# Routed experts in a fused two-block kernel: turns of 128 and of 64 slots alternate in one loop body, and two weight tiles of each 64-slot turn are multiplied as plain fp32

## Reference

```
logits = (xt @ w_router).astype(jnp.float32)
top_vals, top_idx = lax.top_k(logits, TOP_K)                      # TOP_K = 2
top_w = jax.nn.softmax(top_vals, axis=-1)
combine = jnp.sum(jax.nn.one_hot(top_idx, N_EXPERTS) * top_w[..., None], axis=1)
y = jnp.zeros_like(xt)
for e in range(N_EXPERTS):                                        # 8 experts
    y = y + combine[:, e:e + 1] * swiglu(xt, w_gate[e], w_up[e], w_down[e])   # width 3584
```

## Time and profile before

| | us |
|---|---|
| three runs | 2570.8, 2575.92, 2578.6 (median 2575.92) |
| span of the profiled execution | 2569.7 |
| its expert turns (655.03 to 1564.75) | 909.72 |
| a large turn (turns 1, 2, 3) | 119.41 |
| turn 4, small, behind a large one | 105.65 |
| turns 5, 6, 7, small, behind a small one | 108.26, 108.33, 108.84 |

### The profile page before, as it was taken

The page is one execution under the profiler, slowest core; times in us unless marked ns, Lnnn a source line. Parts: engine busy times, 40 slices in busy tenths (PEclk is TensorE's granted clock), DMA queues, the critical chain, the costliest instruction groups (busy, mean ns, idle before and its releaser), DMA issues.

```text
span 2569.7 us, 32436 instructions
## 1 busy us (share of the span) xinstructions
PE 2384.0 (93%) x12064; PEld 1861.5 (72%) x12064; DVE 2009.7 (78%) x3035; ACT 1256.6 (49%) x1302; POOL 285.7 (11%) x305
## 2 busy tenths in 40 slices
PE   9999999999999999999899899999999987878786
PEld 8899999899788888877677678888985443323332
DVE  5766754865898888989999999666668887887875
ACT  2554332363777777878888886216421111111111
POOL 0000000000000000000000000000013433333341
PEclk9999999999999999999999999999999998899999
DMA  8454654541899999999999997531769999999997
GB/s 246 155 189 133 196 193 140 164 159 67 334 375 380 377 375 370 390 374 415 414 415 408 414 416 265 153 92 47 244 248 421 421 421 421 421 422 421 422 421 294
DMA packets 238447, 786.10 MB, mean 306 GB/s; under 512 B 24369, under 2 KB 154545, under 8 KB 162289
## 3 DMA queue, kind: packets, MB, share of 16 engines
q1 hardware_dynamic: 198000, 504.46, 53.1%
q0 software_dynamic: 39184, 276.58, 26.3%
q10 hardware_dynamic: 1136, 3.43, 0.3%
HBM read 777.08 MB, written 7.34 MB: 305 GB/s over the span
## 4 chain that ended last, share of the span: by engine, by line
PE 58%; DMA 22%; DVE 10%; issue 5%; ACT 4%; POOL 0%; DVEq 0%; ACTq 0%; SPq 0%
DMA dense_weights<-in_peer_rows,work 14%; DMA weight_tiles<-in_moe_tiles 7%; PE banks L862 7%; PE banks L864 7%; PE banks L863 7%; PE banks L728 5%; PE banks L1327 5%; PE banks L682 5%; PE banks L683 4%; PE banks L686 4%; PE banks L660 4%; DVE weight_tiles_low L2573 3%; ACT weight_tiles_high L1857 2%; PE banks L592 1%; PE banks L968 1%
## 5 line engine op out<-in xcount | busy, mean ns | idle before, releaser
L2573 DVE TENSOR_TENSOR weight_tiles_low<-weight_tiles,weight_tiles_high 128x2048 fp32r<-128x2048 f32 x335 | 761.5, 2288 | 72.7 <-ACT weight_tiles_high L1857 67.1
L1857 ACT ACTIVATE weight_tiles_high<-weight_tiles 128x2048 fp32r<-128x2048 f32 x332 | 635.5, 1918 | 149.4 <-DMA weight_tiles<-in_moe_tiles 144.7
L1327 PE MATMUL banks<-dense_weights,work 128*128 128x512 f32 x888 | 415.4, 618 | 57.9 <-DVE work L3104 57.5
L1327 PEld LDWEIGHTS banks<-dense_weights,work 128*128 128x128 f32 x888 | 173.0, 199 | 289.9 <-issue 201.1
L3094 DVE CUSTOM_DVE_ANT_0 dense_weights<-dense_weights,banks 128x1024 f32<-128x1024 f32 x222 | 266.5, 1217 | 68.2 <-DMA dense_weights<-in_peer_rows,work 67.3
L2205 DVE TENSOR_TENSOR weight_tiles_low<-weight_tiles,weight_tiles_high 128x2048 fp32r<-128x2048 f32 x93 | 212.2, 2289 | 129.2 <-ACT weight_tiles_high L1623 129.0
L2119 ACT ACTIVATE work<-work,small 128x2 f32<-128x2 f32 x129 | 38.1, 295 | 540.4 <-DVE work L3094 540.2
L1599 POOL DMA_INDIRECT dense_weights<-in_peer_rows,work x222 | 208.6, 940 | 588.0 <-DVE work L3050 315.0
L968 PE MATMUL banks<-weight_tiles_high,gathered_parts 128*128 128x512 f32 x448 | 183.8, 410 | 27.3 <-DVE weight_tiles_low L2573 26.8
L1623 ACT ACTIVATE weight_tiles_high<-weight_tiles 128x2048 fp32r<-128x2048 f32 x93 | 177.4, 1910 | 56.2 <-PE banks L864 29.5
L682 PE MATMUL banks<-weight_tiles_high 128*128 128x256 f32 x800 | 189.4, 281 | 5.1 <-issue 3.1
(11 more groups left out here) (508 smaller groups left out, 4467.9 us busy)
## 6 DMA issues: line engine op xcount, KB each, us to landing
weight_tiles<-in_moe_tiles SPq DMA_DIRECT2D x336, 1024.0 KB, 8.3
weight_tiles<-in_w_in SPq DMA_DIRECT2D x38, 1024.0 KB, 5.5
weight_tiles<-in_w_xkv SPq DMA_DIRECT2D x16, 1024.0 KB, 5.7
weight_tiles<-in_ffn_w_gate SPq DMA_DIRECT2D x11, 1024.0 KB, 5.3
weight_tiles<-in_ffn_w_up SPq DMA_DIRECT2D x11, 1024.0 KB, 5.3
weight_tiles<-in_ffn_w_down SPq DMA_DIRECT2D x11, 1024.0 KB, 5.0
weight_tiles<-in_w_xq SPq DMA_DIRECT2D x8, 1024.0 KB, 5.2
weight_tiles<-in_w_xo SPq DMA_DIRECT2D x8, 1024.0 KB, 5.2
```

The source lines that it names most:

```text
L1327: mm = pe.matmul(halves[half], diag[(first + j) % 8], pair_row(first + j)[:, 1, half * 512:(half + 1) * 512], start=False, stop=end and j ...
L1857: act.activation(high_tile(j), raw_tile(j), ACT.Copy).then_inc(g.high, 1)
L2573: dve.tensor_tensor(low_tile(j), raw_tile(j), high_tile(j).bitcast(F32), ALU.subtract).then_inc(g.split, 1)
```

## The change

1. The order of turns. Turns 0, 2, 4, 6 are large and 1, 3, 5, 7 small. The rank of an expert is turned into its turn: rank r < 4 goes to turn 2r, r > 3 to turn 2r - 7. That is two more small VectorE operations (128x8) ahead of `holds`.
2. The loops. One loop over three pairs, with a large and a small turn in its body, on TensorE, ScalarE and VectorE; the read of `extra_flag` behind it; and the fourth pair written out.
3. Two tiles of each small turn, number 11 (the last of the third gate-up chunk) and number 29 (the second of down), are *whole*: ScalarE and VectorE leave them out, TensorE waits for the raw tile itself and multiplies it as plain fp32, one `matmul` for each of the four pieces, in place of two fp32r ones. They add up in the same PSUM bank.
4. The gather of rows loads 128 rows in a small turn and 64 in a large one (the last turn's too, 128).
5. Counts of semaphores follow (`Turn.parts`, `rows_added`).

```diff
+NATIVE = (11, 29)
+PAIR_PARTS = 2 * EXP_TILES - len(NATIVE)
+class Turn:
+    def whole(self, j):
+        return self.small and j in NATIVE
+    def parts(self, j):
+        return self.parts_before + j + 1 - (sum(i <= j for i in NATIVE) if self.small else 0)
+    def following(self):
+        if self.pair is None:
+            return plain_turn(self.e + 1)
+        return large_turn(self.pair + 1) if self.small else small_turn(self.pair)
...
+                    def unsplit(j, rows_):
+                        pe.wait_ge(g.raw_loads[j % RING], g.loaded_before + 16 * (j // RING + 1) + e * (16 * EXP_TILES // RING))
+                        return raw_tile(j).rearrange("p (k n) -> p k n", k=rows_)
...
+                                    if t.whole(j):
+                                        mm = pe.matmul(bank, xe_high[:, k, :].bitcast(F32), whole[:, i, :], start=(k == 0), stop=(k == KT - 1))
+                                    elif small:
                                         mm = both(bank, xe_high[:, k, :], high[:, i, :], low[:, i, :], k == 0, k == KT - 1)
...
-                    with pe.Fori(0, LARGE) as e:
-                        turn(e, False)
+                    with pe.Fori(0, PAIRS - 1) as p:
+                        turn(large_turn(p))
+                        turn(small_turn(p))
                     pe.wait_ge(routing_ready, 1)
                     overflow = pe.value_load(extra_flag[0:1, 0:1], min_val=0, max_val=1)
-                    with pe.Fori(LARGE, N_EXP) as e:
-                        turn(e, True)
+                    turn(large_turn(PAIRS - 1))
+                    turn(small_turn(PAIRS - 1))
...
-                kind, m = "s_" if e >= LARGE else "", HALF if e + 1 >= LARGE else P
+                kind, m = ("s_", P) if e % 2 else ("", HALF)
...
-                def round_tile(e, j):
-                    wait_used(act, g, e, j)
+                def round_tile(t, j):
+                    if t.whole(j):
+                        return
+                    wait_used(act, g, t.e, j)
...
-                step.then(dve.tensor_tensor(holds, eight(rank, 1), eight(iota8, 2), ALU.is_equal))
+                step.then(dve.tensor_scalar(turn_back, rank, float(LARGE) - 0.5, -float(N_EXP - 1), ALU.is_gt, ALU.mult))
+                step.now(dve.scalar_tensor_tensor(turn_at, rank, 2.0, turn_back, ALU.mult, ALU.add))
+                step.then(dve.tensor_tensor(holds, eight(turn_at, 1), eight(iota8, 2), ALU.is_equal))
...
-                def low_part(e, j):
-                    dve.wait_ge(g.high, e * EXP_TILES + j + 1)
+                def low_part(t, j):
+                    if t.whole(j):
+                        return
+                    dve.wait_ge(g.high, t.parts(j))
                     dve.tensor_tensor(low_tile(j), raw_tile(j), high_tile(j).bitcast(F32), ALU.subtract).then_inc(g.split, 1)
...
-                with dve.Fori(0, LARGE - 1) as e:
-                    expert(e, True)
+                with dve.Fori(0, PAIRS - 1) as p:
+                    expert(large_turn(p), True)
+                    small_expert(small_turn(p), True)
```

More of the change, by code:

```diff
@@ L93, with __init__, large_turn, small_turn @@
 EXP_MARKS = 2 * CHUNKS + DOWN - 1
+PAIRS = N_EXP // 2
+NATIVE = (11, 29)
+PAIR_PARTS = 2 * EXP_TILES - len(NATIVE)
+class Turn:
+    def __init__(self, e, parts_before, pair, small):
+        self.e, self.parts_before, self.pair, self.small = e, parts_before, pair, small
+    def whole(self, j):
[6 more added lines that the diff above has]
+        return large_turn(self.pair + 1) if self.small else small_turn(self.pair)
+def large_turn(p):
+    return Turn(p * 2, p * PAIR_PARTS, p, False)
+def small_turn(p):
+    return Turn(p * 2 + 1, p * PAIR_PARTS + EXP_TILES, p, True)
+def plain_turn(e):
+    return Turn(e, e * EXP_TILES, None, False)
 class Groups:
@@ L561, in wait_used, with rows_added @@
                 eng.wait_ge(used, count + (e - 1) * per)
[L563 to L567, removed]
+        def rows_added(pair, small):
+            return pair * 48 + 16 * (CLEARS + (1 if small else 0))
         block = ctx.enter_context(nc.Block())
@@ L930, in gather, with turn @@
                         g.end(mm, (key, i))
-                def turn(e, small):
+                def turn(t):
+                    e, small = t.e, t.small
                     g.begin_turn(e)
@@ L1011, in turn @@
                             halves.append(g.begin("a", (down_, 1)))
-                        high, low = split(GATE_UP + d, 2)
+                        if t.whole(GATE_UP + d):
+                            whole = unsplit(GATE_UP + d, 2)
+                        else:
+                            high, low = split(GATE_UP + d, 2)
                         for i in range(2):
@@ L1016, in turn @@
                                 n_ = slice(h * 512, (h + 1) * 512)
-                                if small:
+                                if t.whole(GATE_UP + d):
+                                    mm = pe.matmul(halves[h], he_pairs[:, f, :].bitcast(F32), whole[:, i, n_], start=(f == 0), stop=(f == ET - 1))
+                                elif small:
                                     mm = both(halves[h], he_pairs[:, f, :], high[:, i, n_], low[:, i, n_], f == 0, f == ET - 1)
@@ L1899, in small_expert, with expert @@
                         took_it(act.activation(ye[:, h * 512:(h + 1) * 512], bank_in(("s_down", h))[:, :], ACT.Copy, scale=share_here))
-                def expert(e, follow):
+                def expert(t, follow):
+                    e = t.e
                     def done(key):
```

99 lines of the change are left out of this document (52 added, 47 removed).

## The result

The changed kernel takes 2588.75 us (median of 4 runs, 2584.4 to 2592.7), the kernel before 2577.26 us beside it: ratio 1.0051, interval [1.0033, 1.0069]. It is 13 us slower by the ratio. I had said 2575.5 us, and 2588 as the upper end of the range: it is outside. What happened is my second rival, to which I had given 0.2.

What follows compares the result with a forecast made beforehand. It took large turns as bound by TensorE and small ones by DMA; the turns summed to 909.3 us against 909.7, and that -0.4 on the median 2575.92 gave 2575.5 us, range 2561 to 2588.

Steps and rivals of the forecast that it cites:

- my second rival: Loop branch back over two turns: if the body doesn't stay loaded, +11 to +21 us, 2586 to 2597; chance 0.2.
- What bounds the kernel: Expert turns: large ones bound by TensorE (119.41 us), small ones by DMA (108.3 us, 414 GB/s).
- The lag: Tile 0's wait from rounding to multiplication: about 11 us for small turns, 4.8 for large ones.
- the ring: Places for weight tiles: hold 6.3 us more lag than small turns leave, full about half-way through a large turn.
- Turn 0: First large turn: starts as before and takes 120.40 us, the added operations costing 0.
- Small behind large: Each small turn after a large one: 105.65 us plus 1.3 for gathering 128 rows, 106.95, four times.
- Large behind small: Turns 2, 4 and 6: TensorE's 119.41 us plus 0.8 for late tiles after table loads, 120.21 each.
- the sum: All eight turns: 120.40 + 3 x 120.21 + 4 x 106.95 + 0.5 = 909.3 us, against 909.7 before.
- The whole tiles: Two plain fp32 tiles per small turn: 3.4 us each on TensorE against 1.8, covered by DMA, costed at 0.
- The forecast's own range: The time if the forecast's mechanism holds, its gather and start prices varied: 2566 to 2583 us; chance 0.6.
- DMA never rests: Faster rival: small turns behind large ones take 102.0 us, not 105.65; 11 to 16 us gained, 2560 to 2565; chance 0.2.

Runs made afterwards that it cites:

- the alternation alone, written out: Changed kernel with its three loops written out and all 42 tiles of each small turn split (no whole tiles): 2570.64 us, ratio 0.9982 to the kernel before.
- both hints: Changed kernel with a prefetch hint on the back branches of TensorE's and ScalarE's loops, loops kept: 2574.75 us, ratio 0.9996 to the kernel before.
- the last control: The same run as the alternation alone, written out: 2570.64 us, ratio 0.9982, interval 0.9970 to 0.9994.
- the cut kernel: Changed kernel with one product left out of all split tiles of the looped turns, TensorE's loop body 1,535 instructions: 2545.18 us in one run.

## Why the prediction was wrong, step by step

- **What bounds the kernel** was right: large turns 119.6 us with TensorE busy throughout, small ones bound by DMA with 107 us and 410 GB/s. A tile took 10.2 us to land in turn 3 and 7.1 in turn 4, as expected of each kind. The issues of these two turns, in the place of the earlier trace rows:

```profile
weight_tiles<-in_moe_tiles SPq DMA_DIRECT2D x43, 1024.0 KB, 10.2
weight_tiles<-in_moe_tiles SPq DMA_DIRECT2D x41, 1024.0 KB, 7.1
```

- **The lag** of tile 0, read as in the earlier trace rows, is 11.1, 9.1, 8.6 and 11.1 us at turns 1, 3, 5 and 7 of the changed kernel and 6.0 at turn 6; in the alternation alone, written out, it is 10.1 to 11.1 at small turns and 5.8 to 6.4 at large ones. I had said about 11 and 4.8: the ring fills, or nearly, in each large turn, as the forecast had it.
- **Turn 0**: 120.40 said, 120.9 measured. 0.5 off, no part of the question.
- **Small behind large, 106.95**: right. Less the two gaps beyond the ordinary pitch (4.80 and 4.58), turns 1, 3, 5 and 7 are 106.3, 106.8, 107.9 and 106.2. How much of that is the gather of 128 rows was not measured apart.
- **Large behind small, 119.41 + 0.8**: this is the step that failed. The 0.8 was for two table loads; these cost nothing (119.60 with them and both hints). But I had put the loop's start at nothing else. It has two fetches that are not in the earlier trace rows because every body there was short: TensorE's costs some 4.7 us of rest and 1.5 to 2 at the lower clock, twice, and ScalarE's, hidden behind TensorE's in the changed kernel, another 2.1 us twice once TensorE's is gone. 2 x 4.7 + 3.5 = 12.9 us in the turns, less 2.6 by which the sum was else too high, is the 10.3 between 909.3 and 919.6.
- **The whole tiles**: 3.4 us said for one on TensorE. The groups of turns 4 and 5 have 3.6 of busy time for each (x8, 592 ns), and leaving them out changes the time by less than the intervals. Right.

```profile
L1034 PE MATMUL banks<-weight_tiles,gathered_parts 128*128 128x512 f32 x8 | 3.6, 592 | 0.0
L1063 PE MATMUL banks<-weight_tiles,work_parts 128*128 128x512 f32 x8 | 3.6, 592 | 0.0
```

- **The forecast's own range**, 2566 to 2583, is not what its bounds add up to: with 0 for every price the sum gives 2568, with both upper bounds 2586. The measured time is outside of either.
- **The second rival** had the mechanism and the places (turns 2 and 4, not 6), and its 11 to 21 us hold the 12.9. The price was in part luck: it was taken from the landing of a 1 MB tile, 5.4 to 10.7 us a branch, while the rest itself was 4.6 to 4.8 us beyond the ordinary pitch, below that, and the lower clock behind it, which the rival did not have, brought the other 1.5 to 2. What I held against it, that the queue reads ahead and hides a part, is true but worth 1.4 to 1.5 us at a small turn's end. Its chance was too low for an argument that was sound: the body's 2,028 matmuls and weight loads were known, no body of that length was in the trace, and the only case that spoke for "free" had half its length. That "its branch costs nothing" was evidence about 1,177 instructions, not about 2,191. Nor was it true that nothing was known of the price: among TensorE's sequencer records in the trace before stands the branch over the second pass (L1097) with 4.1 us, and its packet of q8 behind it.
- **The Trainium skill** (Runtime: NRT & Kernel Launch, Instruction fetch mechanics) was the one source that spoke of this length. It says that a taken branch whose target isn't in the current window forces a fetch before execution goes on, and the long bodies here agree. The window that it names is two pages, of 256 instructions each; I had read TensorE's room of 2,048 in its place. Neither is the length that a loop may have: 1,544 stayed, 1,704 was fetched again.
- **DMA never rests** (faster, 0.2): small turns behind large ones did not come near 102 us. Refuted; the last control shows a gain of 0.2% (0.3% by the end of its interval), and not that it is the alternation's.

## What to carry to other kernels

Before two steps are put into one loop body, count the instructions of the body on each engine, register ones too, and compare with the longest body that the trace shows to be free (no instruction packets in its later passes). If it is longer, price the branch at several us on every pass, more where the engine is waiting for its inputs and so has nothing queued to hide it; then hint the branch, and look in the profile whether its record has become short, or write the passes out where there are few. When an engine stands at a loop's start and the named releaser was done long before, look at the instruction queues and at the same engine's loop written out.

## What the runs showed of the hardware

- TensorE: bodies of 1,177, 1,535 and 1,544 instructions stay, those of 1,704, 1,876, 1,956, 2,024, 2,191 and 2,356 are fetched again at the branch. ScalarE: the branch over 162 to 178 instructions leaves no wait, that over 331 leaves 2.5 to 2.7 us. VectorE: that over 283 leaves none.
- The fetch holds TensorE's loop branch for 5.5 to 7.5 us while DMA is full with weights. In the changed kernel the packet of 16 KB starts 3.6 to 3.7 us behind the branch's start and takes 0.9 to 1.1 us. How it depends on the load of DMA was not tried.
- After 4.4 to 6 us without matmuls TensorE ran some 4 us at the lower of its two clock levels, which added 1.5 to 2 us to the large turns behind the gaps. After a single rest of 1.7 us it did not; in the cut kernel, where it rested about 1 us ahead of tile after tile, it was at the lower level at 1100.30 too (0.6 us from matmul to matmul).
- A hint at the top of the pass made both loop branches free, at the price of one instruction a pass (TensorE's record 0.4 us). A hint does not always do it: the branch over the second pass has one 5 to 6 us ahead and still took 4.1 to 6.4 us in nine of the 14 profiles, those in which no packet of q8 started between hint and branch.
- The built program loads ScalarE's tables twice at the start of each pass of a loop that holds a large turn (8 loads in the kernel before, 6 in the changed one, 1 where the loop is written out; the kernel before's loop over small turns has none). In the kernel with both hints, where tiles are ahead, they are free.
